# A hybrid attention and expert layer on one core: a modulation chunk shared by two engines, rows of the expert tables spread anew, and a scaling that moves from VectorE to ScalarE

## The reference, cut to what matters

```python
def hybrid_layer(...):                                    # x: (1, 512, 1024), float32
    ada = c @ w_ada + b_ada                               # six vectors of 1024: shift, scale, gate, twice
    h = rms_norm(x, norm1_g) * (1.0 + scale1) + shift1
    z = h @ w_in
    out_a = swa_mixer(...)     # sliding window: 8 query heads, 2 key heads of 64, window of 2 chunks of 64, ALiBi, sink
    out_b = mla_mixer(...)     # latent attention: 8 heads of 96, causal by chunks
    x = x + gate1 * (concatenate([out_a, out_b]) @ w_out)
    h2 = rms_norm(x, norm2_g) * (1.0 + scale2) + shift2
    return x + gate2 * peer_ffn(h2, ...)

def peer_ffn(h, w_query, sub_keys, u_table, v_table):
    q = (xt @ w_query).reshape(T, 8, 2, 64)
    s = jnp.einsum('thpd,hpnd->thpn', q, sub_keys)        # two lists of 128 scores for each of 8 heads
    s_top, i_top = lax.top_k(s, 16)
    cand = (s_top[:, :, 0, :, None] + s_top[:, :, 1, None, :]).reshape(T, 8, 256)
    best, bi = lax.top_k(cand, 16)                        # 8 x 16 = 128 of 16384 experts for each token
    g = softmax(best)
    a = gelu(einsum('tkd,td->tk', u_table[e], x))
    return einsum('tk,tkd->td', g * a, v_table[e])
```

## Time and profile before

| | us |
|---|---|
| median of 3 runs (1462.67 to 1466.7) | 1463.06 |
| the profiled execution | 1464.15 |
| its span | 1462.3 |
| TensorE busy | 1390.9 (95%) |
| VectorE busy | 1200.6 (82%) |
| GpSimd busy | 772.1 (53%) |
| ScalarE busy | 710.3 (49%) |

### The profile page before, as it was taken

How to read it: one execution, slowest core, us unless ns; L and a number is a source line. 1 busy time by engine, 2 the same in 40 slices (tenths; PEclk the granted TensorE clock), 3 DMA queues, 4 the chain that set the end, 5 groups by cost and what they waited for, 6 DMA issues and landing times.

```text
span 1462.3 us, 23449 instructions
## 1 busy us (share of the span) xinstructions
PE 1390.9 (95%) x8415; PEld 1274.4 (87%) x8415; DVE 1200.6 (82%) x2631; ACT 710.3 (49%) x1315; POOL 772.1 (53%) x478
## 2 busy tenths in 40 slices
PE   3999799989999899999999999899999999999997
PEld 1464456867999899999999998899999999999997
DVE  4756786873989889968997874389999999999996
ACT  1235685333444687478835863343443443434331
POOL 2001000211578777878787779855656556555460
PEclk9999799999999999999999999999999999999999
DMA  9920100444779999999999999999999999999995
GB/s 334 325 100 1 58 1 21 153 158 153 276 249 308 337 335 337 403 380 333 333 385 385 324 332 361 369 331 383 388 399 402 399 390 396 390 397 388 387 396 208
DMA packets 158083, 438.79 MB, mean 300 GB/s; under 512 B 16592, under 2 KB 50704, under 8 KB 156816
## 3 DMA queue, kind: packets, MB, share of 16 engines
q1 hardware_dynamic: 91488, 244.55, 46.2%
q0 software_dynamic: 46080, 167.79, 29.9%
q10 hardware_dynamic: 20400, 24.95, 4.8%
HBM read 390.02 MB, written 47.22 MB: 299 GB/s over the span
## 4 chain that ended last, share of the span: by engine, by line
PE 80%; DVE 7%; POOL 4%; DMA 4%; ACT 2%; issue 1%; SPq 1%; ACTq 0%; DVEq 0%; POOLq 0%
PE ps L1228 11%; PE ps L1229 11%; PE ps L1230 11%; PE ps L1177 8%; PE ps L1179 8%; PE ps L1178 8%; PE ps L1188 5%; PE ps L944 5%; POOL lo L552 3%; PE ps L1057 2%; DMA qkc<-in_w_ada 2%; PE ps L1030 1%; DMA rows<-in_u_rows,E 1%; POOL row_res L565 1%; PE ps L1098 1%
## 5 line engine op out<-in xcount | busy, mean ns | idle before, releaser
L801 ACT ACTIVATE hi<-raw 128x1024 fp32r<-128x1024 f32 x256 | 271.2, 1060 | 276.9 <-PE ps L1230 131.4
L552 POOL TENSOR_TENSOR lo<-raw,hi 128x1024 fp32r<-128x1024 f32 x128 | 307.9, 2408 | 143.7 <-ACT hi L801 142.9
L1177 PE MATMUL ps<-h2hi,hi 128*128 128x352 f32 x1024 | 337.1, 329 | 9.6 <-POOL lo L552 9.6
L1179 PE MATMUL ps<-h2hi,lo 128*128 128x352 f32 x1024 | 331.7, 324 | 0.0
L1178 PE MATMUL ps<-h2lo,hi 128*128 128x352 f32 x1024 | 331.3, 324 | 0.0
L1228 PE MATMUL ps<-chi,hi 128*128 128x352 f32 x1008 | 324.2, 322 | 0.0
L1230 PE MATMUL ps<-chi,lo 128*128 128x352 f32 x1008 | 324.1, 322 | 0.0
L1229 PE MATMUL ps<-clo,hi 128*128 128x352 f32 x1008 | 324.1, 322 | 0.0
L565 POOL DMA_INDIRECT row_res<-in_v_tiles,E x91 | 159.0, 1748 | 119.7 <-DVE y_tok L1683 80.8
L1177 PEld LDWEIGHTS ps<-h2hi,hi 128*128 128x128 f32 x1024 | 194.2, 190 | 14.5 <-POOL lo L552 14.2
L1178 PEld LDWEIGHTS ps<-h2lo,hi 128*128 128x128 f32 x1024 | 193.3, 189 | 0.0
(11 more groups left out here) (292 smaller groups left out, 2156.1 us busy)
## 6 DMA issues: line engine op xcount, KB each, us to landing
raw<-in_u_tiles SPq DMA_DIRECT2D x128, 512.0 KB, 5.9
raw<-in_v_tiles SPq DMA_DIRECT2D x128, 512.0 KB, 7.5
gelus<-act_out ACTq DMA_DIRECT2D x128, 176.0 KB, 5.6
act_in<-gelus SPq DMA_DIRECT2D x128, 176.0 KB, 9.0
gates<-stage SPq DMA_DIRECT2D x32, 512.0 KB, 8.7
gate<-gates SPq DMA_DIRECT2D x32, 512.0 KB, 9.1
late<-in_w_ada SPq DMA_DIRECT2D x4, 2048.0 KB, 7.9
qkT<-in_w_ada SPq DMA_DIRECT2D x3, 2048.0 KB, 21.2
```

The source lines that it names most:

```text
L552: nc.gpsimd.tensor_tensor(lo[m % 3][:], raw[m % 3][:], hi[m % 3][:].bitcast(F32), ALU.subtract).then_inc(u_lo, 1)
L801: nc.scalar.activation(hi[m % 3][:], raw[m % 3][:], ACT.Copy).then_inc(t_hi, 1)
L1177: nc.tensor.matmul(out, hi[n % 3][:, cols], dense(h2hi, k), start=(k == 0), stop=False)
L1179: last = nc.tensor.matmul(out, lo[n % 3][:, cols], dense(h2hi, k), start=False, stop=(k == KD - 1))
```

## The change

It has five edits.
1. The chunk ("ada", 1) is halved: TensorE forms the row of its first 256 columns, and VectorE sums the other 256 (`modulate_half`, eight instructions, after `modulate` of the second prepared chunk and ahead of `modulation(1, 2)`); TensorE sums these over partitions once `half_done` is set.
2. In the sliding units VectorE scales only the first head; ScalarE scales the second (`scale_second`), between exponentials(u+1) and copy_pt(u). TensorE's transposes wait for both.
3. `FILL` is 9, 11, 12 instead of 12, 10, 10. Four of the row sums stand before `weigh(0)`, the other 156 in steps 0 to 123 of the second pass; before, 160 stood in steps 0 to 127. `more_at` is one step earlier.
4. The gelu of the row dots is written to PSUM bank 1, and the product with the weights reads it there.
5. x1 is loaded back in two halves, the first (blocks 4 to 7) when all but five row uses are done, the second after the last. The last loops run over blocks 4 to 7, then 0 to 3.

```diff
+        def row_cols(j):
+            return CH if j == direct[0] else CH // 2
-        FILL, PAUSES, MORE = {1: 12, 2: 10, 3: 10}, 15, 4
+        FILL, PAUSES, EARLY, LAST = {1: 9, 2: 11, 3: 12}, 15, 4, NT - 4
-        sums_at = [n for n in range(NT) for _ in range(2 if n % MORE == MORE - 1 else 1)][:SU]
-        more_at = tail_at + 3 + (SU - SLOTS) // 2
-        row_step = row_step[:SLOTS] + [tail_at + 2 + j // 2 for j in range(SU - SLOTS)] + [NT + n for n in sums_at]
+        sums_at = [j * LAST // (SU - EARLY) for j in range(SU - EARLY)]
+        more_at = tail_at + 2 + (SU - SLOTS) // 2
+        row_step = row_step[:SLOTS] + [tail_at + 2 + j // 2 for j in range(SU - SLOTS)] + \
+            [more_at + 1 + j // 2 for j in range(EARLY)] + [NT + n for n in sums_at]
+        D_LAST = tuple(range(KD // 2, KD)) + tuple(range(KD // 2))
...
+            sp.wait_ge(x1_out, 16)
+            sp.wait_ge(row_used, 2 * SU - 5)
+            sp.dma_start(res[:, KD // 2:KD, :], x1[:, KD // 2:KD, :]).then_inc(x1_in[0], 16)
             sp.wait_ge(row_used, 2 * SU)
-            sp.dma_start(res[:], x1).then_inc(x1_in, 16)
-            for d in range(KD):
-                sp.wait_ge(y_sb, d + 1)
+            sp.dma_start(res[:, 0:KD // 2, :], x1[:, 0:KD // 2, :]).then_inc(x1_in[1], 16)
+            for i, d in enumerate(D_LAST):
+                sp.wait_ge(y_sb, i + 1)
...
+            def scale_second(u):
+                nk = len(key_tiles(*units[u][:2])) * P
+                act.wait_ge(r_ready, u + 1)
+                v = pb[:, u % 4, 1, 256 - nk:256]
+                nc.scalar.activation(v, v, ACT.Copy, scale=rsm[:, u % 4, 1:2]).then_inc(p_second, 1)
             for u in range(NU):
                 if u + 1 < NU:
                     exponentials(u + 1)
+                if u < NSU:
+                    scale_second(u)
                 copy_pt(u)
...
                 if n == more_at:
                     act.wait_ge(row_used, SU)
-                    nc.scalar.activation(cc[:], aa[:], ACT.Gelu).then_inc(aa_gelu, 1)
+                    nc.scalar.activation(ps[:, 1, 0:SU], aa[:], ACT.Gelu).then_inc(aa_gelu, 1)
...
             def modulation_turned(j):
+                if row_cols(j) < CH:
+                    pe.wait_ge(half_done, 1)
+                for q in range(row_cols(j) // P, CH // P):
+                    nc.tensor.matmul(ada_at(j * (CH // P) + q), accs[:, 0, q * P:(q + 1) * P], ones[:, 0:1], start=True, stop=True)
                 pe.wait_ge(ada_row_sb, direct.index(j) + 1)
...
                 pe.wait_ge(p_ready, u + 1)
+                if kind == "s":
+                    pe.wait_ge(p_second, u + 1)
...
+            def modulate_half(j):
+                n = place["ada", j]
+                at, before = slot[n]
+                cols = slice(row_cols(j), CH)
+                dve.wait_ge(chunk_in[at], 16 * (before + 1))
+                dve.wait_ge(ada_done, 1)
+                sums = accs[:, 0, cols]
+                settled(nc.vector.tensor_scalar(sums, chunk(n)[:, 0, cols], cT[:, 0:1], None, ALU.mult))
+                for k in range(1, KD):
+                    settled(nc.vector.scalar_tensor_tensor(out=sums, in0=chunk(n)[:, k, cols], scalar=cT[:, k:k + 1],
+                                                           in1=sums, op0=ALU.mult, op1=ALU.add))
+                dve.sem_inc(half_done, 1)
+
+            modulate_half(direct[1])
...
-                settled(nc.vector.reciprocal(rsm[:, u % 4, 0:nj], sm[:, u % 4, 0:nj]))
-                for j in range(nj):
+                nc.vector.reciprocal(rsm[:, u % 4, 0:nj], sm[:, u % 4, 0:nj]).then_inc(r_ready, 1)
+                dve.wait_ge(r_ready, u + 1)
+                for j in range(1):
...
-            tt_(cc[:], cc[:], wg[:], ALU.mult).then_inc(cc_ready, 1)
+            tt_(cc[:], ps[:, 1, 0:SU], wg[:], ALU.mult).then_inc(cc_ready, 1)
+            for n in range(EARLY):
+                row_sum(n)
             weigh(0)
```

More of the change, by code:

```diff
@@ L209, in build @@
         shift_ready = sem("shift_ready")
+        half_done = sem("half_done")
         h_scaled = sem("h_scaled")
@@ L240, in build @@
         p_ready = sem("p_ready")
+        r_ready = sem("r_ready")
+        p_second = sem("p_second")
         pt_ps = sem("pt_ps")
@@ L280, in build @@
         x1_out = sem("x1_out")
-        x1_in = sem("x1_in")
+        x1_in = [sem(f"x1_in{b}") for b in range(2)]
         more_ready = sem("more_ready")
@@ L402, in build @@
         assert len(row_step) >= SLOTS
-        sums_at = [n for n in range(NT) for _ in range(2 if n % MORE == MORE - 1 else 1)][:SU]
-        more_at = tail_at + 3 + (SU - SLOTS) // 2
-        row_step = row_step[:SLOTS] + [tail_at + 2 + j // 2 for j in range(SU - SLOTS)] + [NT + n for n in sums_at]
+        sums_at = [j * LAST // (SU - EARLY) for j in range(SU - EARLY)]
+        more_at = tail_at + 2 + (SU - SLOTS) // 2
+        row_step = row_step[:SLOTS] + [tail_at + 2 + j // 2 for j in range(SU - SLOTS)] + \
+            [more_at + 1 + j // 2 for j in range(EARLY)] + [NT + n for n in sums_at]
         assert len(row_step) == 2 * SU
+        D_LAST = tuple(range(KD // 2, KD)) + tuple(range(KD // 2))
+        assert [(2 * SU - j) % NROWS for j in (7, 6)] == [5, 6]
         x_tok = ps[:, 4:6, :].rearrange("p a c -> p (a c)")
@@ L904, in modulation_row @@
                 for k in range(KD):
-                    last = nc.tensor.matmul(row_ps(j), cT[:, k:k + 1], chunk(n)[:, k, :], start=(k == 0), stop=(k == KD - 1))
+                    last = nc.tensor.matmul(row_ps(j)[:, 0:row_cols(j)], cT[:, k:k + 1], chunk(n)[:, k, 0:row_cols(j)],
+                                            start=(k == 0), stop=(k == KD - 1))
                 last.then_inc(ada_row, 1)
             def modulation_turned(j):
+                if row_cols(j) < CH:
+                    pe.wait_ge(half_done, 1)
+                for q in range(row_cols(j) // P, CH // P):
+                    nc.tensor.matmul(ada_at(j * (CH // P) + q), accs[:, 0, q * P:(q + 1) * P], ones[:, 0:1], start=True, stop=True)
                 pe.wait_ge(ada_row_sb, direct.index(j) + 1)
-                for q in range(CH // P):
-                    col = j * (CH // P) + q
-                    last = nc.tensor.matmul(ada_at(col), ada_rows(j)[:, q * P:(q + 1) * P], ones[0:1, 0:1],
+                for q in range(row_cols(j) // P):
+                    last = nc.tensor.matmul(ada_at(j * (CH // P) + q), ada_rows(j)[:, q * P:(q + 1) * P], ones[0:1, 0:1],
                                             start=True, stop=True)
@@ L1236, in _ @@
             pe.wait_ge(c_lo, NT)
-            for d in range(KD):
+            for d in D_LAST:
                 cols = slice(d * P, (d + 1) * P)
@@ L1708, in _ @@
                     if at == n:
-                        row_sum(j)
+                        row_sum(EARLY + j)
                 if n + 3 < NT:
                     low_c(n + 3)
-            dve.wait_ge(x1_in, 16)
-            for d in range(KD):
-                dve.wait_ge(y_ps, NT - 2 + d + 1)
+            for i, d in enumerate(D_LAST):
+                if i % (KD // 2) == 0:
+                    dve.wait_ge(x1_in[i // (KD // 2)], 16)
+                dve.wait_ge(y_ps, NT - 2 + i + 1)
                 nc.vector.scalar_tensor_tensor(out=res[:, d, :], in0=ps[:, d, :], scalar=ada[:, 5 * KD + d:5 * KD + d + 1],
```

4 lines of the change are left out of this document (2 added, 2 removed).

## The result

The changed kernel takes 1468.43 us (median of 12 executions) where the kernel before, timed beside it, takes 1463.88: a ratio of 1.0041, 95% interval 1.0029 to 1.0052. It is slower by 4.5 us, where 2.9 us faster was forecast. The time lies 3 us above the range.

A forecast was written before the change was run, and what follows sets the result against it. It took TensorE's matmuls as the bound (80% of the chain), edits counting only where the chain leaves TensorE. The terms 0.2 + 5.3 - 4.5 + 2.4 - 6.3 gave -2.9 us: 1460.2 us for the median, range 1452.5 to 1465.5.

The forecast's parts named there:

- the cover of the moved dots: Searches 2 and 3: moved dots fit into VectorE's waits before `eS` and cost nothing; without that cover 3.4 us.
- the time of the four early sums: End of the first pass: sums take about 5.0 us plus one or two `lo`; `weigh(0)` at 953 to 957.4.
- modulation chunk: Before the first projection: TensorE's half is earlier, VectorE becomes the late one; +0.2 us, ends -0.3 and +0.6.
- scaling on ScalarE: Sliding attention units: ScalarE's second-head scaling lengthens a round through TensorE; +5.3 us, ends +3.5 and +6.4.
- `FILL`: First search: three row dots fewer cut TensorE's wait and half the clock's price; -4.5 us, bounds -2.5 to -6.7.
- gelu and early sums: End of the first pass: `cc` gets short, but four row sums delay `weigh(0)`; +2.4 us, ends 0 and +3.2.
- tail: Kernel's end: sums finish earlier, x1 halves are hidden, the last loop runs without a stop; -6.3 us, ends -7.0 and -4.0.
- The steady unit: Sliding units at full clock: 2.72 us each, 0.34 more than today, nine units 3.1 us.
- the first seven units: Sliding units with TensorE at 1.2 GHz: part of the longer round is hidden; +1.7 us, between 0 and 2.4.
- rival B: Sliding units: ScalarE's scaling is hidden and units follow VectorE, 4.0 us saved; 1450.9 us, chance 0.18.
- VectorE's load per step is as before: Second pass: 156 sums in 124 steps, 1.26 a step against 1.25, finished before the expert loop ends.
- Rival D: Sliding units keep TensorE at 1.2 GHz, +9.5 us, 1464.4; five latent units at that clock give 1468.4; chance 0.08.

The follow-up runs named there:

- e1: The changed kernel again, nothing edited, for a second profile: 1467.54 us, ratio 1.0035 to the kernel before.
- e7: The kernel before with only the row dots spread anew over the searches, 9, 11, 12: 1461.33 us, ratio 0.9988.
- e2: The changed kernel, but VectorE scales both heads of a sliding unit as before: 1460.52 us, ratio 0.9991 to the kernel before.
- e3: The kernel before with only the second head's scaling moved to ScalarE, behind the exponentials: 1471.12 us, ratio 1.0075.
- e4: The changed kernel with no row sum ahead of `weigh(0)`, all 160 in steps 0 to 123: 1462.18 us, ratio 1.0008 to the kernel before.
- e8: The kernel before with only the edits of the end: 160 sums in steps 0 to 123, x1 in two halves, blocks 4 to 7 first: 1458.59 us.
- e6: The kernel before with the second head's scaling on ScalarE, placed ahead of the next unit's exponentials: 1462.77 us, ratio 0.9999.
- first profile: The first profiled execution of the changed kernel, nothing edited: 1479.66 us, 11 us above the median.
- e5: The changed kernel with VectorE scaling both heads and no row sum ahead of `weigh(0)`: 1455.87 us, ratio 0.9947 to the kernel before.
- e12: The changed kernel with no early sums and ScalarE's scaling ahead of the exponentials: 1453.44 us, ratio 0.9939 to the kernel before.
- e9: The changed kernel with VectorE scaling both heads, no early sums, and 160 row sums in steps 0 to 115: 1464.35 us, ratio 1.0012.
- e10: The changed kernel with VectorE scaling both heads, no early sums, and 160 row sums in steps 0 to 126: 1455.88 us, ratio 0.9950.

## Why the prediction was wrong

It forecast -2.9 us as a sum of five terms. Two of them came out beyond the bounds given for them: the cover of the moved dots (`FILL`) and the time of the four early sums. The other three kept to their bounds in the profiles. By the profiles these two make 4.7 of the 4.9 us between the forecast and the sum of the measured terms (+2.0); by the medians the scaling and the tail add 1.7 and 1.8 us. By term, in the profiles of e1 and e7 and in the medians:

| term | forecast | profile | median of the experiment |
|---|---|---|---|
| modulation chunk | +0.2 | +0.4 | not run alone |
| scaling on ScalarE | +5.3 | +5.9 | +7.0 (e1 - e2), +8.8 (e3) |
| `FILL` | -4.5 | -2.1 | -1.7 (e7) |
| gelu and early sums | +2.4 | +4.7 | +5.4 (e1 - e4) |
| tail | -6.3 | -6.9 | -4.5 (e8), second pass included |

The profile's value of the early sums is the +5.4 of the hand-over less the 1.1 that e7 has there without them, and the 0.4 of the second pass.

**Modulation: right.** 3.61 us for TensorE's half, the order of VectorE as told, 44.92 where 44.7 was forecast.

**Scaling: right in its mechanism, somewhat small in its size.** The steady unit was forecast at 2.72 us and is 2.74, waiting for ScalarE's new line; the scaling takes 0.50 (0.49 was taken). The mis-sized term is the first seven units: forecast +1.7, measured 20.13 us (159.16 to 179.29) against 17.29, +2.8. TensorE stays at 1.2 GHz until 176.2 here, 174.6 in the profile of before and 172.7 in e2. e6 shows that it was the round through TensorE, not ScalarE's load. For rival B the Trainium skill ("Perfetto Trace Analysis", section "Optimizing Scalar/DVE Operations") says that offloading a saturated VectorE to ScalarE may make sense; here it does with the scaling ahead of the exponentials (2.12 us a unit) and does not behind them (2.74).

**FILL: the step that failed is the cover.** The gain in search 1 came in full, 4.4 us and the clock behind it. But the text said that dots moved to searches 2 and 3 "fit and cost nothing" in the waits before `eS`. On VectorE they do: it still waits 7.2 us (e1) and 8.2 us (e7) for `eS` in search 2 with the eleventh dot (6.0 before). What the step left out is GpSimd. "one of them now waits for the dots ... ahead of a `lo`" was written without a price, and about the end of search 1; the gather that costs stands some 45 us before the end of search 2. It waits 4.9 us for its buffer, `lo` behind it is late, and TensorE waits 2.2 us, then 1.7 (0.9 in e7) at the end of the search. The bounds of -2.5 to -6.7 held only what VectorE does; the measured -2.1 lies outside.

**Early sums: the step that failed is the time of the four sums.** The text gave 5.0 us and one or two `lo`, and took +2.4 of at most +3.2. Measured from `cc` to `weigh(0)`: 949.84 to 961.54, 11.7 us, near the upper bound (5.0 + 2.4 + 4.7 = 12.1), and `cc` itself ran at 946.8, counted from the third `turn_slots` as before, and not at 945.3. So `weigh(0)` came at 958.5, beyond the latest time allowed for (957.4). Two costs behind that were left out: TensorE's clock, at 1.2 GHz from 964.7 to 968.1 after its wait, makes the last dot last 5.5 us instead of 3.9, and the gelu after it waits for its output buffer (2.67 us of TensorE's time at the start of the second pass in the first profile, 0.4 in e1). For the lock the Trainium skill ("SBUF — State Buffer", section "Who interferes with whom") calls the ports that the two engines share an exclusive lock, and says that a VectorE instruction with two SBUF inputs contends with a GpSimd instruction that reads SBUF. 9.36 us for three sums around a `lo` pair of 4.73 agrees, and so does 0.32 for `cc` from PSUM during a `lo`. That a faster `cc` is worth nothing to TensorE is seen between e7 (old `cc`, 167.0 us from the third `turn_slots` to the first mix) and e4 and e5 (new, 166.9 and 167.1).

**Tail: right** for the end, 6.9 for 6.3, the additions 1.3 us apart behind TensorE. "VectorE's load per step is as before" was nearly true, 1.26 rows for 1.25, and left out the loads: with all 160 sums in 124 steps a v tile can land late (e8). In the changed kernel itself, with 156 sums there, TensorE waits for no late tile in e1.

**Rival D** named half clock in the sliding and latent units. Its 1468.4 us is the measured median by chance: a usual execution has no half clock in its latent units. A rare one has it in the latent units, +13.9 and +13.8 us in the two profiles that show it (first profile, e4). Of the 38 executions of kernels with the scaling behind the exponentials (the changed kernel, e1, e3, e4) four lie 11 to 15 us above the median of their kernel, with a granted clock of 0.975 to 0.980 over the whole execution (0.983 to 0.987 in the other 34). Of the 63 of the other experiments the highest is 6.6 above its median, of the 77 of the kernel before 4.4. Luck alone would put all four among the 38 about twice in a thousand times. That ties it to this edit, but not to the place of the scaling: e6 and e12 together have only 15 executions. What sets it off in one execution and not in the next stays open: the profiles of e1 and e4 are alike until 200 us, with half clock up to 176.2 and 176.3.

## What to carry to other kernels

Before an operation moves to an emptier engine, write down that engine's order and ask which of its instructions waits for another engine behind the new one: the same scaling cost 7 us behind the exponentials and nothing ahead of them. Where an engine's queue holds gathers between its computations, price each gather's wait for its buffer as a wait of what stands behind it. Work with two SBUF operands on VectorE beside GpSimd's belongs to where nobody waits for VectorE, and before loads are packed closer, compare the bytes per time that they will ask for with the most that the trace carries over as long a stretch.

## What was not expected of the hardware

In e9 the DMAs of one core carried 398 to 401 GB/s over 400 us with a busy share of 1.03, loads of 512 KB and gathers mixed; 1.38 rows a step asked for 408, and steps came late. Over 5 us 416 are seen. The Trainium skill ("DMA: Bandwidth & Descriptors", section "Specifications") gives about 358 GB/s as the limit of HBM for a core and 435 as a ceiling; the measurement lies between them, and it decides here.

In the first profile TensorE's clock was at 1.2 GHz for 34 us in which TensorE was busy for 33.73. What it did just before is alike in e1, where the clock stayed at 2.4 GHz: from 176 to 200 us it was busy for 16.24 us in the first profile and 16.25 in e1 (19.83 before). And a wait of 2.22 us ahead of 963.15 was followed by half clock in e1, while one of 2.22 ahead of 589.54 in e7 was followed by none, and the same wait in e10 (2.23 ahead of 589.51) was. So a wait of this length costs its own time, and in some executions the clock's besides.
